# A two-layer hybrid transformer on one NeuronCore: experts interleaved on TensorE, attention and indexer heads in two row halves, a table scatter moved into a branch

## The chip, the core and the metric

One core of a Trainium2 chip. Everything is float32. The metric is the device time of one execution of the whole program in microseconds (us), smaller is better. TensorE (PE in the profile) multiplies, VectorE (DVE), ScalarE (ACT) and GpSimd (POOL) do the elementwise work, SyncE (SP) issues the large DMA loads, and POOL issues the indirect ones. SBUF is the on-chip memory, PSUM holds the results of TensorE in eight banks.

## The reference, cut to what matters

512 tokens of width 1024 pass two layers: a mixer, a layer norm, a mixture of experts, a layer norm and a gated injection. Layer 0 mixes by retention and pooling, which the change doesn't touch. Layer 1 mixes by sparse attention:

```python
sc = relu(einsum('bqhd,bsd->bqhs', q_idx, k_idx))     # indexer: 8 heads of 64
I = einsum('bqh,bqhs->bqs', w_idx, sc)                # causal; the top 128 keys are kept
logits = q . k * 64**-0.5 - slopes[h] * (t - idx)     # 16 heads of 64, kept keys alone
o = softmax(logits) @ v
```

Each layer's mixture has 32 experts of 1024 x 1024 (gate and up) and 512 x 1024 (down) weights; each token goes to two of them:

```python
h = xt[tok] @ w_gu[e];  a, b = split(h, 2)
y[row] += gate * ((silu(a) * b) @ w_down[e])
```

## The kernel before

The program is a list of blocks, each with one instruction stream for each engine and a barrier at its end: retention, output projection, routing (`route`), experts (`experts`), injection; then `latents` (indexer and latent projections of layer 1), `attention`, and again output projection, routing, experts, injection. Nothing is planned by a scheduler: the order on each engine is the order written, and semaphores join the engines.

**Experts.** Every expert gets 64 slots. SP streams the weights of an expert into one of two areas q = 0, 1 (experts 2i+q): three loads of 2 MB, the two halves of the gate and up weights (gu) and the down weights (dn). The loads of the next expert of an area are written in the order gu half 0, gu half 1, dn of q = 0, then the same of q = 1, and each waits for the matmuls that free its place (`s_gu_half`, `s_gu`, `s_dn`). Experts 0, 1 and the gate and up weights of expert 31 (in w3, w4) are in place before the block; the down weights of expert 31 come by `load_last_dn` into XT, once the second gather has landed. The last four places of the sequence run experts 31, 28, 29, 30. `one(q, i)` is written alike for TensorE, ScalarE and VectorE, and takes one expert from start to end on each before the next:

- TensorE transposes the gathered rows (L875), multiplies gate and up in two halves (L890), transposes the gated product (L897), multiplies down (L904). A token row is split in two column halves, which run in the two halves of TensorE's columns.
- ScalarE copies the transposed rows (L909), does silu (L913) and scales the result (L1195). VectorE multiplies (L916) and copies the transposed product (L919).
- GpSimd gathers a row list by indirect DMA (L863) and scatters the result (L869).

Before its second round of gathers GpSimd also writes `table` (L1120): eight indirect scatters of 128 entries of 16 bytes, which only the branch for overfull experts (`Further`, more than 64 tokens) reads. The branch isn't entered with this input: the trace holds 64 results of experts (L1195), 32 for each layer.

**Latents.** TensorE multiplies four chunks of indexer queries (L1468), and after them the scores of two heads for three row tiles (L1478). Key and query tiles hold two heads in 128 partitions; KI is kept twice, each with the other head's half zeroed, so that a score product contracts 128 rows. Two PSUM banks take the scores in turn. ScalarE rectifies (L1552), VectorE accumulates (L1616), then picks the top 128 (L1631, L1635) while TensorE goes on with the latents (L1508) and the projections (L1537).

**Attention.** 64 units (t, h): row tile t with (t + 1) * 128 keys, head h. A unit is a score product on TensorE (L1707, again 128 rows with zeroed halves of QH, two banks), slope and mask on VectorE (L1752), the row maximum (L1755), exp on ScalarE (L1775), the reciprocal on VectorE (L1739), the division on GpSimd for even units (L1795) and on VectorE for odd ones (L1745), transposes on TensorE (L1716), a copy on ScalarE (L1783) and, for two heads together, the product with the values (L1728). Transposes run 4 units and value products 6 units behind the scores.

## Time and profile before

| | us |
|---|---|
| median of three runs | 1728.17 (1726.48 to 1731.79) |
| the profiled execution | 1732.38 |
| its span, first to last instruction | 1730.5 |
| PE busy in it | 1455.4 |
| experts of layer 0, first to last product | 255.4 to 742.6 |
| experts of layer 1 | 1149.6 to 1635.9 |
| latents and attention | 838 to 1057 |

The profiled execution has 1.9 us around its span and is 4.2 us above the median, so that differences are taken from it and set against the median. DMA rates count all 16 engines of the core. A timeline row gives the start, the duration, the engine, the line and operation, the operands and the count of merged instructions; in brackets stands the idle time before it and what ended that. A float32 product of up to 512 columns shows as two MATMUL records.

### The profile page before, as it was taken

Reading aid. Unit: us, or ns where it says so; the run is one execution under the profiler, and the core shown is the slowest. Engines: PE = TensorE matmul, PEld = TensorE weight load, DVE = VectorE, ACT = ScalarE, POOL = GpSimd, SP = SyncE. Lnnn points to the kernel's source line nnn. Section 1 sums busy time; section 2 is a strip of 40 time slices with the busy share of each in tenths; the row PEclk is TensorE's granted clock in tenths of the full one; section 3 lists DMA queues with packets and bytes.
Section 4 is the critical chain, followed back from the end, with each engine's and each line's share of the span. In section 5 each row is a group of like instructions: output and inputs, shape, how many; then the busy total and the mean of one; then the engine's idle time right before and its main releaser. Section 6 shows DMA issues by size and latency. Waiting matters only on the chain. (4 is left out here: it accounts for less than half of the span.)

```text
span 1730.5 us, 16759 instructions
## 1 busy us (share of the span) xinstructions
PE 1455.4 (84%) x5992; PEld 662.9 (38%) x5992; DVE 407.3 (24%) x972; ACT 317.1 (18%) x656; POOL 219.7 (13%) x319
## 2 busy tenths in 40 slices
PE   7998968877877878869999999968878778788698
PEld 5885542222222223234444565532222222222243
DVE  3425340000000000044167584330000000000062
ACT  3211011101011010122234673011010100101121
POOL 0000012111111111100001241031111111111000
PEclk9999969999999999989999999969999999999989
DMA  7108159999999999854200004389999999999450
GB/s 271 49 25 333 67 195 294 428 429 430 427 429 430 429 428 429 327 222 179 103 0 1 1 1 189 122 243 384 429 429 428 430 429 429 429 429 410 200 207 37
DMA packets 78808, 482.44 MB, mean 279 GB/s; under 512 B 18912, under 2 KB 20964, under 8 KB 45992
## 3 DMA queue, kind: packets, MB, share of 16 engines
q1 hardware_dynamic: 65800, 463.76, 66.0%
q0 software_dynamic: 10752, 16.85, 2.7%
q10 hardware_dynamic: 2208, 1.20, 0.2%
q8 instruction: 28, 0.46, 0.1%
q14 instruction: 20, 0.16, 0.0%
HBM read 474.91 MB, written 23.63 MB: 288 GB/s over the span
## 5 line engine op out<-in xcount | busy, mean ns | idle before, releaser
L890 PE MATMUL PS<-wide,w 128*64 128x512 f32 x1984 | 454.9, 604 | 83.7 <-ACT w L909 44.5
L890 PEld LDWEIGHTS PS<-wide,w 128*64 128x64 f32 x1984 | 134.5, 138 | 361.7 <-issue 225.0
L904 PE MATMUL PS<-slim,w 128*64 128x512 f32 x992 | 238.4, 624 | 38.8 <-DVE w L919 38.8
L916 DVE TENSOR_TENSOR w<-w,PS 128x256 f32<-128x256 f32 x64 | 27.0, 421 | 872.5 <-ACT w L913 872.5
L904 PEld LDWEIGHTS PS<-slim,w 128*64 128x64 f32 x992 | 75.5, 142 | 158.8 <-issue 109.1
L913 ACT ACTIVATE w<-PS 128x256 f32<-128x256 f32 x64 | 24.6, 384 | 511.3 <-PE PS L890 511.3
L1305 PE MATMUL PS<-wide,XT 128*128 128x512 f32 x256 | 111.5, 592 | 0.0
L1195 ACT ACTIVATE w<-PS,w 128x512 f32<-128x512 f32 x64 | 44.0, 687 | 360.8 <-PE PS L904 360.8
L1112 POOL COPY w<-w 128x1 uint32 (+1 forms) x64 | 11.7, 183 | 702.0 <-ACT w L1195 702.0
L897 PE MATMUL PS<-ident,w 128*128 128x128 f32 x128 | 32.3, 334 | 60.2 <-DVE w L916 54.5
L863 POOL DMA_INDIRECT w<-x_rows,w x64 | 67.6, 1056 | 56.9 <-POOL w L1105 55.6
L869 POOL DMA_INDIRECT y_rows<-w x64 | 65.2, 1019 | 55.1 <-POOL w L1112 55.1
L1305 PEld LDWEIGHTS PS<-wide,XT 128*128 128x128 f32 x256 | 48.0, 190 | 57.4 <-issue 57.4
L897 PEld LDWEIGHTS PS<-ident,w 128*128 128x128 f32 x128 | 20.1, 206 | 116.5 <-DVE w L916 116.5
L637 PE MATMUL PS<-wide,slim 128*128 128x512 f32 x128 | 56.0, 594 | 1.1 <-PEq L1698 1.1
L875 PEld LDWEIGHTS PS<-ident,w 128*128 128x128 f32 x256 | 36.0, 209 | 54.3 <-issue 49.6
L875 PE MATMUL PS<-ident,w 128*128 128x128 f32 x256 | 48.6, 313 | 3.5 <-DMA w<-x_rows,w 3.5
L1707 PE MATMUL PS<-w,wide 128*128 128x128 f32 (+3 forms) x128 | 48.1, 460 | 1.5 <-PEq L1458 0.9
L169 ACT ACTIVATE XT<-PS 128x512 f32<-128x512 f32 x40 | 21.7, 594 | 139.5 <-PE PS L162 139.5
L1795 POOL TENSOR_SCALAR w<-w 128x128 f32<-128x128 f32 (+3 forms) x32 | 35.5, 1110 | 91.6 <-DVE w L1739 91.6
L405 PE MATMUL PS<-x_high,w_high 128*128 128x512 f32 x96 | 38.2, 398 | 7.9 <-DVE w_low L343 7.9
L909 ACT ACTIVATE w<-PS 128x512 f32<-128x512 f32 x64 | 37.8, 591 | 31.9 <-PE PS L875 31.8
(221 smaller groups left out, 1545.8 us busy)
## 6 DMA issues: line engine op xcount, KB each, us to landing
wide<-in_moe_w_gu SPq DMA_DIRECT2D x124, 2048.0 KB, 26.5
slim<-in_moe_w_down SPq DMA_DIRECT2D x62, 2048.0 KB, 26.6
w<-in_moe_w_gu SPq DMA_DIRECT2D x4, 2048.0 KB, 19.4
w<-y_rows SPq DMA_DIRECT2D x16, 512.0 KB, 9.1
wide<-in_ple_w_gate SPq DMA_DIRECT2D x4, 2048.0 KB, 13.6
w<-in_ab_w_in SPq DMA_DIRECT2D x2, 2048.0 KB, 13.9
w_in<-in_ab_w_in SPq DMA_DIRECT2D x2, 2048.0 KB, 7.7
x_rows<-X SPq DMA_DIRECT2D x8, 512.0 KB, 3.0
```

Of the source, the lines that this page charges most:

```text
L405: m = pe.matmul(PS[:, j % 8, :], lhsT, rhs, start=(k == 0 and r == 0), stop=(k == KD - 1 and r == 2))
L637: m = pe.matmul(PS[:, 2 * t + c, :], mixed[:, k, t * P:(t + 1) * P], w_halves[c][:, k, :], start=(k == 0), stop=(k == KD - 1))
L863: pool.indirect_dma_start(out=xg[q], out_offset=None, in_=x_half, in_offset=bass.IndirectOffsetOnAxis(ap=index, axis=0), bounds_check=2 * ...
L869: pool.indirect_dma_start(out=y_rows, out_offset=bass.IndirectOffsetOnAxis(ap=index, axis=0), in_=ys[q], in_offset=None, bounds_check=4 * ...
L875: m = pe.transpose(PS[:, q, c * P:(c + 1) * P], xg[q].rearrange("p (f c) -> p c f", c=4)[:, c, :], ident[:, :])
L890: m = pe.matmul(PS[u * SLOTS:(u + 1) * SLOTS, 2 + q, :], xeT[q][:, k, :], gu[k].rearrange("p (a u c) -> p a u c", a=2, u=2)[:, :, u, :], s ...
L897: m = pe.transpose(PS[:, 4 + q, c * P:(c + 1) * P], ga.rearrange("p (f c) -> p c f", c=2)[:, c, :], ident[:, :])
L904: m = pe.matmul(PS[u * SLOTS:(u + 1) * SLOTS, 6 + q, :], gT[:, k, :], dn[k][:, u * NB:(u + 1) * NB], start=(k == 0), stop=(k == FF // P - 1))
L909: return act.activation(xeT[q].rearrange("p (u c) s -> p c u s", u=2), PS[:, q, :].rearrange("p (c u s) -> p c u s", c=4, u=2), ACT.Copy)
L1195: act.activation(ys[q], PS[:, 6 + q, :], ACT.Copy, scale=R["gate_of"][:, bass.ds(expert(q, i), 1)]).then_inc(s_y[q], 1)
L1305: m = pe.matmul(PS[:, 2 + u % 6, :], XT[:, k, t * P:(t + 1) * P], wg[:, k, c * NB:(c + 1) * NB], start=(k == 0), stop=(k == KD - 1))
L1707: pe.matmul(PS[:, j % 2, 0:width[t]], QH[:, h % 2, h // 2, t * P:(t + 1) * P], KH[:, h // 2, 0:width[t]], start=True, stop=True).then_inc( ...
```

## The change

- `experts`: TensorE and ScalarE take two experts interleaved. Where TensorE had `one(0, i)`, `one(1, i)`, it now runs `up(0,i)`, `out(1,i-1)`, `back(0,i)`, `turn(1,i)`, `up(1,i)`, `out(0,i)`, `back(1,i)`, `turn(0,i+1)`. The streams of VectorE, of SP's expert loads and of GpSimd's gathers and scatters keep their order.
- The eight table scatters move into the branch for overfull experts. `load_last_dn` moves into the routing block, without its wait.
- `latents`: KI is kept once; the two heads of a chunk are multiplied in rows 0 to 63 and 64 to 127; the scores take four banks, and the two heads of a tile follow one another. Four zeroings on GpSimd go.
- `attention`: QH too is kept once and score products contract 64 rows; four score banks; slope, mask and maximum in one VectorE instruction (`tensor_tensor_reduce`), with the sign and slope folded into QH's scale; transposes 6 and value products 8 units behind; GpSimd divides three units of four, VectorE copies one transposed unit of four.

```diff
 # route
+                @block.sync
+                def _(sp):
+                    load_last_dn(sp, l)
 # experts, SP
-                    sp.wait_ge(s_gath[1], 16)
-                    load_last_dn(sp, l)
 # experts, GpSimd: moved into further.pool(pool, more, fill_table)
-                    pool.wait_ge(s_place, 1)
-                    for c in range(2 * T):
-                        pool.indirect_dma_start(
-                            out=table, ...).then_inc(s_tab, 16)
 # experts, TensorE (ScalarE: gate(0,i), scale(1,i-1), take(1,i), gate(1,i), scale(0,i), take(0,i+1))
-                        one(0, i)
-                        one(1, i)
+                    def pair_of(i, first=False):
+                        up(0, i)
+                        if not first:
+                            out(1, i - 1, first=isinstance(i, int) and i == 1)
+                        back(0, i)
+                        turn(1, i)
+                        up(1, i)
+                        out(0, i, first)
+                        back(1, i)
 # latents
-            units = [(t, h) for h in range(IH) for t in SEL]
+            units = [(t, 2 * c + u) for c in range(IH // 2) for t in SEL for u in range(2)]
-                            if i >= 2:
-                                pe.wait_ge(s_relu, i - 1)
-                            pe.matmul(PS[:, 6 + i % 2, 0:width[t]], QI[:, h // 2, t * P:(t + 1) * P],
-                                      KI[:, h % 2, 0:width[t]], start=True, stop=True).then_inc(s_is, 1)
+                            if i >= 4:
+                                pe.wait_ge(s_relu, i - 3)
+                            hd = slice((h % 2) * HD, (h % 2 + 1) * HD)
+                            pe.matmul(PS[:, 4 + i % 4, 0:width[t]], QI[hd, h // 2, t * P:(t + 1) * P],
+                                      KI[hd, 0:width[t]], start=True, stop=True).then_inc(s_is, 1)
 # attention
-            LAG_R, LAG_T, LAG_V = 1, 4, 6
+            LAG_R, LAG_D, LAG_T, LAG_V = 2, 3, 6, 8
+            divider = [1 if j % 4 == 3 else 0 for j in range(N)]
+            copier = [1 if j % 4 == 1 else 0 for j in range(N)]
+                                pe.matmul(PS[:, j % 4, 0:width[t]], QH[hd, h // 2, t * P:(t + 1) * P],
+                                          KH[hd, h // 2, 0:width[t]], start=True, stop=True).then_inc(s_s, 1)
-                        dve.scalar_tensor_tensor(g, DMASK[t], -slope[h], PS[:, i % 2, 0:width[t]],
-                                                 ALU.mult, ALU.add).then_inc(s_l, 1)
-                        dve.tensor_reduce(nmax[:, i:i + 1], g, AX.X, ALU.max, negate=True).then_inc(s_max, 1)
+                            dve.tensor_tensor_reduce(LG[i % LGS][:, 0:width[t]], PS[:, i % 4, 0:width[t]], DMASK[t],
+                                                     SLOPE[h], -LOWEST, ALU.add, ALU.min,
+                                                     nmax[:, i:i + 1]).then_inc(s_l, 1)
```

## Rows read from the trace of the kernel before

**Rows 1.** Page, span in 40 equal slices of 43 us: DMA busy in tenths, rate.

```profile
DMA  7108159999999999854200004389999999999450
GB/s 271 49 25 333 67 195 294 428 429 430 427 429 430 429 428 429 327 222 179 103 0 1 1 1 189 122 243 384 429 429 428 430 429 429 429 429 410 200 207 37
```

**Rows 2.** Busy time by windows: an expert stretch, and attention's last tile.

```profile
core 0: us, PE busy (x) PEld busy (x) DVE busy (x) ACT busy (x) POOL busy (x), PEclk, DMA share, GB/s
300.00:400.00 100.00, 80.05 (x360) 27.17 (x358) 5.07 (x12) 10.46 (x20) 17.16 (x28) 1.00 1.01 428
...
1020.00:1048.00 28.00, 28.00 (x199) 17.40 (x200) 24.53 (x55) 20.08 (x49) 12.39 (x8) 1.00 0.01 1
```

**Rows 3.** Timeline, layer 0: second gate-and-up halves of experts 3 and 27.

```profile
305.19 3.65 PE L890 MATMUL PS<-wide,w 128*64 128x512 f32 x16 [0.38 <-DMA wide<-in_moe_w_gu]
...
675.02 3.65 PE L890 MATMUL PS<-wide,w 128*64 128x512 f32 x16 [0.88 <-DMA wide<-in_moe_w_gu]
```

**Rows 4.** Timeline, end of layer 0's experts: expert 28, and the last down product.

```profile
701.73 7.09 PE L890 MATMUL PS<-wide,w 128*64 128x512 f32 x32 [0.69 <-ACT w L909]
...
709.75 0.50 PE L897 MATMUL PS<-ident,w 128*128 128x128 f32 x2 [0.94 <-DVE w L916]
...
710.77 3.65 PE L904 MATMUL PS<-slim,w 128*64 128x512 f32 x16 [0.52 <-DVE w L919]
...
738.91 3.65 PE L904 MATMUL PS<-slim,w 128*64 128x512 f32 x16 [0.52 <-DVE w L919]
```

**Rows 5.** Timeline, start of layer 0's experts: first and last table scatter, loads.

```profile
253.99 1.02 POOL L1120 DMA_INDIRECT table<-w  x1 [0.30 <-issue]
...
255.40 9.95 PE L890 MATMUL PS<-wide,w 128*64 128x512 f32 x32 [0.69 <-ACT w L909]
255.46 0.38 SPq L442 DMA_DIRECT2D XT<-in_moe_w_down  x1
...
262.17 3.77 SPq L429 DMA_DIRECT2D wide<-in_moe_w_gu  x2
...
262.98 0.96 POOL L1120 DMA_INDIRECT table<-w  x1 [0.31 <-issue]
...
271.20 0.39 SPq L433 DMA_DIRECT2D slim<-in_moe_w_down  x1
```

**Rows 6.** DMA view of 244 to 284 us, 40 slices of 1 us; median landing.

```profile
DMA  9999300040409175999999866998999716999559
GB/s 426 410 442 385 147 0 8 0 135 4 127 2 115 16 115 205 451 419 405 247 223 107 66 66 66 148 115 99 99 82 98 82 33 296 353 201 111 107 213 426
...
table<-w POOLq DMA_INDIRECT x8, 11.8
```

**Rows 7.** Table scatters of layer 0 (240 to 330 us), issue to landing.

```profile
DMA to landing us min/median/max: 4.4/11.8/18.7
```

**Rows 8.** Timeline, latents: score stretches, and the next long stretch.

```profile
858.03 2.68 PE L1478 MATMUL PS<-w 128*128 128x256 f32 x8
...
862.58 7.03 PE L1468 MATMUL PS<-XT,wide 128*128 128x512 f32 x16
...
880.86 2.68 PE L1478 MATMUL PS<-w 128*128 128x256 f32 x8
...
890.32 27.63 PE L1508 MATMUL PS<-wide,XT 128*128 128x512 f32 x64
```

**Rows 9.** Timeline, attention: first scores of t = 1, 2, 3, value products, last pair.

```profile
979.60 0.70 PE L1707 MATMUL PS<-w,wide 128*128 128x256 f32 x2
...
997.49 0.91 PE L1707 MATMUL PS<-w,wide 128*128 128x384 f32 x2
...
1020.71 1.12 PE L1707 MATMUL PS<-w,wide 128*128 128x512 f32 x2
...
1033.85 1.09 PE L1728 MATMUL PS<-w,XT 128*64 128x128 f32 x16
...
1046.32 1.13 PE L1707 MATMUL PS<-w,wide 128*128 128x512 f32 x2
```

**Rows 10.** Groups by line and form: the row maximum at 512 keys.

```profile
L1755 DVE TENSOR_REDUCE w<-w 128x1 f32<-128x512 f32 x16 | 11.0, 686 | 0.5
```

More of the change, by code:

```diff
@@ L998, in dve, with pool @@
                 self.run(dve, count, body, s["dve"], before)
-            def pool(self, pool, count):
+            def pool(self, pool, count, before):
                 s = self.s
@@ L1006, in body @@
                     scatter(pool, 1, put1[1], s["scat"])
-                self.run(pool, count, body, s["pool_end"])
+                self.run(pool, count, body, s["pool_end"], before)
             def pe(self, pe, count):
@@ L1132, in _, with fill_table, turn, up @@
                             put_rows(q, i)
-                    pool.wait_ge(s_tab, 16 * 2 * T)
                     for q in range(2):
                         pool.wait_ge(s_scat[q], 16 * PAIRS)
-                    further.pool(pool, more)
+                    def fill_table():
+                        pool.wait_ge(s_place, 1)
+                        for c in range(2 * T):
+                            pool.indirect_dma_start(
+                                out=table, out_offset=bass.IndirectOffsetOnAxis(ap=R["place"][:, c:c + 1], axis=0),
+                                in_=R["entry"][:, c, :], in_offset=None).then_inc(s_tab, 16)
+                        pool.wait_ge(s_tab, 16 * 2 * T)
+                    further.pool(pool, more, fill_table)
                 @block.tensor
                 def _(pe):
-                    def one(q, i, first=False):
-                        a, loads = area(q, i)
+                    def turn(q, i):
                         pe.wait_ge(s_gath[q], 16 * i + 16)
                         turn_gathered(pe, q).then_inc(s_turn[q], 1)
+                    def up(q, i):
+                        a, loads = area(q, i)
                         pe.wait_ge(s_xe[q], i + 1)
@@ L1150, in one, with back, out @@
                             gate_up(pe, q, last_gu if a is None else gu_of[a], half).then_inc(done[q], 1)
+                    def back(q, i):
                         pe.wait_ge(s_gated[q], i + 1)
                         turn_gated(pe, q).then_inc(s_gturn[q], 1)
+                    def out(q, i, first=False):
+                        a, loads = area(q, i)
                         pe.wait_ge(s_gt[q], i + 1)
@@ L1180, in _, with take, gate @@
                 def _(act):
-                    def one(q, i, first=False):
+                    def take(q, i):
                         act.wait_ge(s_turn[q], i + 1)
                         copy_gathered(act, q).then_inc(s_xe[q], 1)
+                    def gate(q, i, first=False):
                         act.wait_ge(s_gu[q], i + 1)
@@ L1189, in one, with scale @@
                         silu(act, q).then_inc(s_silu[q], 1)
+                    def scale(q, i, first=False):
                         act.wait_ge(s_dn[q], i + 1)
@@ L1196, in one, with pair_of @@
                                        scale=R["gate_of"][:, bass.ds(expert(q, i), 1)]).then_inc(s_y[q], 1)
-                    one(0, 0, first=True)
-                    one(1, 0, first=True)
+                    def pair_of(i, first=False):
+                        gate(0, i, first)
+                        if not first:
+                            scale(1, i - 1, first=isinstance(i, int) and i == 1)
+                        take(1, i)
+                        gate(1, i, first)
+                        scale(0, i, first)
+                    take(0, 0)
+                    pair_of(0, first=True)
+                    take(0, 1)
+                    pair_of(1)
                     more = further.count(act)
-                    with act.Fori(1, END) as i:
-                        one(0, i)
-                        one(1, i)
+                    with act.Fori(2, END) as i:
+                        take(0, i)
+                        pair_of(i)
                     for i in (END, END + 1):
-                        one(0, i)
-                        one(1, i)
+                        take(0, i)
+                        pair_of(i)
+                    scale(1, END + 1)
                     further.act(act, more)
@@ L1421, in build @@
         m8 = {1: w2[:, 3376:3384], 2: w2[:, 3384:3392], 3: w2[:, 3392:3400]}
+        SLOPE = [2.0 ** (-8.0 * (h + 1) / AH) for h in range(AH)]
         SEL = list(range(1, T))
```

170 lines of the change are left out of this document (82 added, 88 removed).

## The prediction

> **What bounds the kernel now.** I read the page's slices first: in two long stretches the DMA engines are busy throughout at 429 GB/s, and between them lies a stretch with hardly any transfer [rows 1]. The windows say who works there. In the experts TensorE is busy 80 of 100 us while the DMA share is 1.01: the weight stream is the bound. In the last tile of attention TensorE is busy 28.0 of 28 us, VectorE 24.5, ScalarE 20.1, GpSimd 12.4: TensorE is the bound, VectorE close behind [rows 2].
>
> The timeline gives the two rates that matter in the experts. From the second gate-and-up half of expert 3 to that of expert 27, both released by a landing weight load, are 369.8 us for 24 experts: 15.4 us each, or 5.14 us for each 2 MB load with the gathers and scatters beside it [rows 3]. Where no load is waited for, at the end, two experts lie between the down products at 710.77 and 738.91: 14.07 us each [rows 4]. So TensorE's own rate is only 1.3 us better than the stream's, and a TensorE order that is faster still gains nothing in the middle. It can gain at the two ends alone: when the stream starts, and after it stops.
>
> **Experts, middle.** In the interleaved order the idle 0.93 us before L897 (the wait for silu and product) and 0.52 us before L904 [rows 4] lie behind another expert's product. The wait for the copied rows (0.69 us) stays, since turn still stands directly before up. TensorE's own rate becomes 14.07 - 0.93 - 0.52 = 12.6 us an expert, under 15.4: worth 0 here. The cover for that is the DMA stream; without it the edit would give 1.45 us an expert.
>
> But the order of releases changes, and SP's order doesn't. A dn place used to be free about 6 us after its expert's second half; now out(q) runs after the other expert's up. With the second half of expert (0,i) landing at 0: half 3.65, out(1,i-1) to 7.3, back and turn and copy, first half of the next at 10.3 (its load landed), second half at 15.4 (load) to 19.1, out(0,i) to 22.7. Only then may SP issue dn(0), and the two gu halves behind it in SP's queue, whose places have been free for some us, go with it. The stream works until 30.8 on what was issued before (expert (0,i+1)'s halves end there), so the three loads arrive some 8 us before the queue is dry. The same margin holds for the other area. I take 0, and keep the dry queue as a rival.
>
> **Experts, start.** Here is the largest single thing in the trace. From 263 to 282 us the DMA engines are busy and move only about 140 GB/s, 20 slices that sum to 2812 GB/s of a possible 8600 [rows 6]; 13.5 us of stream are lost. The table scatters are issued from 254.0 to 263.0 [rows 5] and take up to 18.7 us to land, hence until about 281.7 [rows 7]: the slow stretch ends as they do. The gathers and scatters of every expert run in the middle too, at 428 GB/s [rows 2], so they aren't the cause. With the table out, the stream runs at 5.14 us a load, and the releases decide. The first up starts at 255.4, its first half frees its place at 262.2, its end is at 265.35 [rows 5]. Then wait and back to 266.8, turn and copy 1.4 to 268.2, up(1,0) 7.1 to 275.3, out(0,0) to 279.0, against a dn load issued at 271.2 before. The two gu halves of expert 2 land by about 274, the queue is dry until 279.0, and three loads from about 280.5 end at 296 to 296.5: the second half of expert 3 is there, which before started at 305.19 [rows 3, 5]. Gain 8.7 us, I take 8.5 for each layer (layer 1 has the same eight scatters), 17 in all. Bounds: 0 if the slow stretch stays; 15.8 if the queue never went dry (262.2 + 1.5 + 5 x 5.14 = 289.4).
>
> `load_last_dn` in routing adds 5 us of stream there. The engines are idle from 249 [rows 6], so it moves into empty time, until about 253. The first gathers now share the engines with it and TensorE waits for the first of them (L875): I put 1 us on it for each layer, bounds 0 and 2, loss 2 in all. GpSimd loses eight scatters, which frees its gather of the third expert, not waited for.
>
> **Experts, end.** After up of expert 27, before: 0.93 + 0.5 + 0.52 + 3.65, then four experts of 14.07: 61.9 us to the end of the last down. After: out of 26 and back 4.15, four of 12.7, then 0.5 and the last out 3.65: 59.1 [rows 4]. The last dn load is released after out(1,14) and still lands 7 us before its use. Gain 2.8 a layer, 5.6 in all. Bounds: 0 (a late last load) and 4.3.
>
> **Latents.** A single full-row product costs 27.63/64 = 0.43 us for each record, 0.86 at 512 columns [rows 8]. The four chunks of scores cost TensorE 4.55, 4.55 and 9.46 us (862.58 - 858.03; 890.32 - 880.86). Two heads in two row halves should run at once, as the two column halves of the value products do: 16 records of 128 columns in 1.09 us, where one after the other at 0.107 they would take 1.7 [rows 9]. A chunk is 2304 columns; at half, 1.9 us and some 0.2. But ScalarE and VectorE have to follow, with two relu tiles: I put chunks 0 and 1 at 3.0 each, and 2 and 3 together at 6.5: 3.1 + 3.0 = 6.1 less. VectorE's selection starts that much earlier, nearly, so the third wait in the latents moves along; I take 5.5, bounds 2 and 7. The zeroings were on GpSimd beside longer TensorE work: 0.
>
> **Attention.** A pair of units takes (997.49 - 979.60)/8 = 2.24 us at t = 1, 2.90 at t = 2, and (1046.32 - 1020.71)/7 = 3.66 at t = 3 [rows 9]. Two heads at once save half of four records, less 0.06 for one more switch of the tile shape: at t = 3 0.80, t = 2 0.58, t = 1 0.37; at t = 0, where the engines wait for one another, I take 0.2 to 0.3. Eight pairs of each: 6.4 + 4.6 + 3.0 + 2.0 = 16. The others must keep up with the 2.86 us a pair at t = 3, which is 22 us for what the window of 28 us holds. VectorE drops a reduction of 0.69 us for each of its 15 units [rows 10], 24.5 - 10.3, plus a few copies: 15. GpSimd's half becomes three quarters: 12.4 x 1.5 = 18.6. ScalarE gives copies away: under 20.1. All fit, GpSimd and ScalarE narrowly. The deeper lags add one round of transposes and value products at the end, 1 us. Gain 15. What the fused instruction costs, no row shows: between one pass (0.69) and two (1.37) [rows 10]. At two, VectorE would need 25 us of the window and bind: 5 us of the 15 gone. I take one pass, as it reads each operand once. Bounds of the whole term: 0 (row halves don't overlap) and 20 (the four banks also remove the waits at t = 0 and 1).
>
> What a change of tile shape costs is seen at the value products, which have one at either end: 1.09 us for 16 records, of which 8 slots of 0.107 are 0.86, so at most 0.23 for switches and the pipeline's tail together [rows 9]. The Trainium skill speaks against this part: its page TensorEngine Tiling (Array Packing), section Key Properties, says that changing the tiling mode, unlike changing the tile, drains TensorE. By the row the term stays at 15; by the rule, with a drain of 0.23 at each end of every pair of scores, 36 pairs would lose up to 16 and nothing would be left, which is the second rival's end.
>
> **Sum.** 17 - 2 + 5.6 + 5.5 + 15 = 41 us off the profiled 1732.4 (span 1730.5 and 1.9 around it), hence 1691 for such an execution; the median of before is 4.2 lower, so 1728.2 - 41 = 1687.
>
> **Rivals.**
> - The slow stretch stays, since something else in it is slow (the load into XT, the first results): nothing is gained at the starts, 1728.2 - 24 = 1704. For it: the last load was in flight there too. Against: it ends as the last table scatter lands. The Trainium skill, page DMA: Bandwidth & Descriptors, section Specifications, has transfers under 512 B done by read-modify-write, and the scatter's entries have 16 B; the trace agrees with the forecast's side, by the 140 GB/s. 0.10.
> - The row halves don't overlap, or the switch or the fused instruction eats it: latents and attention give 2 to 5 instead of 20, 1710. For it: no row shows row halves. Against: the column halves. 0.13.
> - The engines keep step better than I count (four banks, longer lags), 50 to 60 less: 1673. 0.10.
> - Slower: the queue of loads runs dry in the middle, as dn and the next two halves now go out together. Of 58 streamed experts each has to lose 0.71 us to cancel the 41; at 1.0 us the time is 1728 - 41 + 58 = 1745. Against: 8 us of margin. 0.06.
> - The forecast: 0.61.
>
> **How the numbers follow.** The forecast's own range is 1675 to 1700, from the bounds of its terms. To hold 8 of 10 the range takes in the first two rivals nearly, and a part of the third: 1668 to 1708. A difference under 0.3% (5 us) is about what a measurement of this kernel can't tell from none. Faster by more than that: the first, second, third and last case, less their tails, 0.90. Slower by more: 0.05, the dry queue. Within: 0.05.
>
> **What would show it.** In the DMA slices no stretch of busy engines at 100 to 200 GB/s after the first expert; the second half of expert 3 some 41 us after the first up started, instead of 50; in the middle 15.4 us an expert, DMA share 1.0; down products at the end some 12.7 us apart; pairs in attention of 2.9 us at t = 3; L1508 about 6 us earlier after the first L1468. The prediction is wrong if a slow stretch remains, if the middle takes more than 15.6 us an expert, or if score pairs last as long as before.

## The result and the profile after

The changed kernel takes 1711.24 us against 1729.98 us for the kernel before on the same chip (medians of 4 each), a ratio of 0.989 with a 95% interval of 0.986 to 0.992. It is faster, by 19 us where 41 were forecast (1687, range 1668 to 1708), so the time lies above the range. One execution of the four took 2482 us at a granted clock of 0.55 and is left out of the ratio; the median of the other three is 1709.62.

The profiled execution took 1709.62 us (span 1707.7). Its page, the slices that answer to [rows 1] and the clock above them:

```profile
PEclk8999969999999999989999699969999999999989
DMA  7107267999999999883200004378999999999650
GB/s 275 50 26 306 100 240 290 429 430 428 427 425 428 427 428 423 328 312 129 104 1 1 1 2 178 124 304 360 430 429 428 427 424 426 426 413 421 255 209 37
```

The two streams are as fast as before, and the clock line of the changed kernel has a 6 at slice 22 (from 939 to 982 us), counted from 0. The other two 6s are in the page of before too, where slice 22 has a 9.

**Start of the experts.** The DMA view of 244 to 284 us, 40 slices of 1 us, as [rows 6]:

```profile
DMA  9999999984000030009399999999910000098999
GB/s 442 426 410 442 426 426 418 434 357 164 0 0 0 0 90 0 0 0 229 98 393 442 410 459 426 426 459 393 393 66 16 0 0 0 0 147 336 401 410 459
```

The stretch at 140 GB/s is gone. The last down load fills the time to 253. Between 274 and 279 the queue is dry. The timeline of TensorE, then of SyncE's queue, as [rows 5]:

```profile
254.27 1.13 PE L879 MATMUL PS<-ident,w 128*128 128x128 f32 x4 [4.12 <-DMA w<-x_rows,w]
256.09 8.61 PE L894 MATMUL PS<-wide,w 128*64 128x512 f32 x32 [0.69 <-ACT w L913]
...
274.24 3.60 PE L908 MATMUL PS<-slim,w 128*64 128x512 f32 x16
...
292.77 8.78 PE L894 MATMUL PS<-wide,w 128*64 128x512 f32 x32 [0.69 <-ACT w L913]
```

```profile
278.08 0.39 SPq L433 DMA_DIRECT2D slim<-in_moe_w_down  x1
278.77 1.35 SPq L429 DMA_DIRECT2D wide<-in_moe_w_gu  x2
```

The first row shows a wait of 4.12 us for the first gather. The same row of the kernel before:

```profile
253.58 1.13 PE L875 MATMUL PS<-ident,w 128*128 128x128 f32 x4 [1.87 <-DMA w<-x_rows,w]
```

In layer 1 the wait is 3.39 us, and was 1.12. The moved load is in flight as the gather is issued; v_lastdn below tests that it is the cause. Expert 3's up ends at 301.55, so its second half began about 3.65 earlier, at 297.9, 41.8 us after the first up (49.8 before).

**Middle and end of the experts.** Timeline of TensorE, as [rows 3, 4]:

```profile
399.34 8.75 PE L894 MATMUL PS<-wide,w 128*64 128x512 f32 x32 [2.17 <-DMA wide<-in_moe_w_gu]
407.92 3.60 PE L908 MATMUL PS<-slim,w 128*64 128x512 f32 x16
411.46 0.51 PE L901 MATMUL PS<-ident,w 128*128 128x128 f32 x2
...
712.85 7.09 PE L894 MATMUL PS<-wide,w 128*64 128x512 f32 x32 [0.69 <-ACT w L913]
719.77 3.60 PE L908 MATMUL PS<-slim,w 128*64 128x512 f32 x16
723.30 0.50 PE L901 MATMUL PS<-ident,w 128*128 128x128 f32 x2
724.32 3.65 PE L908 MATMUL PS<-slim,w 128*64 128x512 f32 x16 [0.52 <-DVE w L923]
```

Transposes and down products have lost their waits, save the last; the saved time is now the wait for the load, and a part of it goes into a lower clock (0.94 from 300 to 400 us, 1.00 before), which the stream covers. The last down product ends 14.6 us earlier than before (727.97 against 742.56). Of that 1.7 us is no effect of the change: in the profiled execution of before one down product of this stretch took 5.35 us instead of 3.65, at a granted clock of 0.83 from 680 to 690 us:

```profile
680.93 5.35 PE L904 MATMUL PS<-slim,w 128*64 128x512 f32 x16 [0.82 <-DVE w L919]
```

**Latents**, as [rows 8]: the score chunks (the first and the last two together are shown) take 2.5, 2.5 and 6.79 us between long products, where they took 4.55, 4.55 and 9.46.

```profile
845.71 2.57 PE L1520 MATMUL PS<-w 64*128 64x256 f32 x12
848.21 7.13 PE L1509 MATMUL PS<-XT,wide 128*128 128x512 f32 x16
...
864.83 6.86 PE L1520 MATMUL PS<-w 64*128 64x256 f32 x24
871.62 3.70 PE L1550 MATMUL PS<-wide,XT 128*128 128x512 f32 x8
```

**Attention.** Windows (columns as in [rows 2], the granted clock is the figure before the DMA share) of its first part, and of its last tile:

```profile
940.00:960.00 20.00, 17.39 (x69) 8.68 (x67) 5.32 (x44) 11.16 (x40) 3.35 (x9) 0.89 0.00 0
960.00:980.00 20.00, 18.67 (x81) 9.33 (x80) 8.05 (x48) 9.55 (x38) 4.29 (x10) 0.50 0.00 1
...
1020.00:1048.00 28.00, 24.88 (x226) 16.67 (x225) 12.56 (x42) 15.91 (x35) 6.70 (x9) 1.00 0.06 7
```

From 960 to 980 us TensorE ran at its lower level, 1.2 GHz; before, the clock was 1.00 throughout. The timeline at t = 3, as [rows 9]:

```profile
1025.52 1.13 PE L1749 MATMUL PS<-w,wide 64*128 64x512 f32 x4
1026.58 1.09 PE L1758 MATMUL PS<-ident,w 128*128 128x128 f32 x8
1027.60 1.09 PE L1770 MATMUL PS<-w,XT 128*64 128x128 f32 x16
1028.62 1.13 PE L1749 MATMUL PS<-w,wide 64*128 64x512 f32 x4
1029.68 0.66 PE L1758 MATMUL PS<-ident,w 128*128 128x128 f32 x4
1031.29 0.63 PE L1758 MATMUL PS<-ident,w 128*128 128x128 f32 x4 [0.95 <-DVE w L1782]
1031.85 1.09 PE L1770 MATMUL PS<-w,XT 128*64 128x128 f32 x16
1032.87 1.13 PE L1749 MATMUL PS<-w,wide 64*128 64x512 f32 x4
```

Four score records now take what two took. One pair goes through in 3.10 us, the next in 4.25, with a wait for a PSUM copy of VectorE in it (L1782). Such waits sum to 9.0 us in attention.

The spans of the two profiled executions differ by 22.8 us; that is 4 more than the medians, since the one of before is above its median and the one of the changed kernel below. The table splits them at the starts of six TensorE records in the two timelines (first up of layer 0; its last down; first and last score of attention; first up of layer 1; its last down; and the end of the span):

| stretch | before | after | difference | forecast |
|---|---|---|---|---|
| up to the first up | 255.4 | 256.1 | +0.7 | +1 |
| experts, layer 0 | 486.6 | 471.3 | -15.3 | -11.3 |
| injection, latents | 225.4 | 223.3 | -2.1 | -5.5 |
| attention's scores | 80.7 | 82.7 | +2.0 | -15 |
| last values, layer 1's start | 101.4 | 105.3 | +3.9 | +1 |
| experts, layer 1 | 485.8 | 474.8 | -11.0 | -11.3 |
| rest | 95.2 | 94.2 | -1.0 | 0 |

The terms for the experts were met or passed, the one for attention missed by 17 and the one for the latents by 3.4. The first experiments ask where each lies.

### The profile page after: what moved, and what is told of

Read it like the earlier page. It is cut to its first block and busy times, and to the rows that moved or that the text cites. A ratio compares the mean times of both kernels' runs of the same rounds, so it can differ in the third digit from the quotient of the medians.

```text
span 1707.7 us, 16740 instructions
## 1 busy us (share of the span) xinstructions
PE 1453.6 (85%) x5992; PEld 670.6 (39%) x5992; DVE 379.9 (22%) x972; ACT 315.9 (18%) x640; POOL 188.0 (11%) x315
## 5 line engine op out<-in xcount | busy, mean ns | idle before, releaser
L894 PE MATMUL PS<-wide,w 128*64 128x512 f32 x1984 | 499.4, 655 | 148.6 <-DMA wide<-in_moe_w_gu 138.8
L894 PEld LDWEIGHTS PS<-wide,w 128*64 128x64 f32 x1984 | 157.2, 149 | 448.4 <-issue 364.1
L908 PE MATMUL PS<-slim,w 128*64 128x512 f32 x992 | 223.6, 592 | 1.0 <-DVE w L923 1.0
L923 DVE COPY w<-PS 128x256 f32<-128x256 f32 x64 | 27.2, 425 | 188.6 <-PE PS L901 188.6
L879 PE MATMUL PS<-ident,w 128*128 128x128 f32 x256 | 42.8, 291 | 10.5 <-DMA w<-x_rows,w 10.5
L1834 POOL TENSOR_SCALAR w<-w 128x128 f32<-128x128 f32 (+3 forms) x48 | 26.5, 554 | 136.3 <-DVE w L1798 135.9
L1818 ACT ACTIVATE w<-w 128x128 f32<-128x128 f32 (+3 forms) x64 | 35.6, 556 | 31.9 <-DVE w L1792 31.9
L879 PEld LDWEIGHTS PS<-ident,w 128*128 128x128 f32 x256 | 36.8, 210 | 11.5 <-DMA w<-x_rows,w 11.5
## 6 DMA issues: line engine op xcount, KB each, us to landing
wide<-in_moe_w_gu SPq DMA_DIRECT2D x124, 2048.0 KB, 17.9
slim<-in_moe_w_down SPq DMA_DIRECT2D x62, 2048.0 KB, 13.4
```

Of the source, the lines that this page charges most:

```text
L879: m = pe.transpose(PS[:, q, c * P:(c + 1) * P], xg[q].rearrange("p (f c) -> p c f", c=4)[:, c, :], ident[:, :])
L894: m = pe.matmul(PS[u * SLOTS:(u + 1) * SLOTS, 2 + q, :], xeT[q][:, k, :], gu[k].rearrange("p (a u c) -> p a u c", a=2, u=2)[:, :, u, :], s ...
L908: m = pe.matmul(PS[u * SLOTS:(u + 1) * SLOTS, 6 + q, :], gT[:, k, :], dn[k][:, u * NB:(u + 1) * NB], start=(k == 0), stop=(k == FF // P - 1))
L923: return dve.tensor_copy(gT.rearrange("p (u c) s -> p c u s", u=2), PS[:, 4 + q, 0:2 * P].rearrange("p (c u s) -> p c u s", c=2, u=2))
L1818: act.activation(g, g, ACT.Exp, bias=nmax[:, i:i + 1], scale=-1.0, accum_out=rsum[:, i:i + 1]).then_inc(s_p, 1)
```

## The experiments

Each time below is the median of its executions, with the ratio to the kernel before on the same chip. That kernel's median there was 1732.4 for the four runs whose names begin with e, 1731.7 for v_serial, v_sporder, v_lastdn and v_copyfirst, 1730.9 for v_repeat, v_pool_one, b_two and b_all, and 1731.1 for the last three. Durations of stretches are read as in the table, from one profiled execution each. How far they can be trusted is seen at b_all and b_all_repeat below: the experts' code is the same, and their experts differ by 3 us a layer.

### One part of the change at a time

e_experts is the changed kernel with the latents and attention of before, e_attention the kernel before with the changed latents and attention. e_table is the kernel before with one edit:

```
# e_table, GpSimd, before.py + this only
-  pool.wait_ge(s_place, 1)
-  for c in range(2 * T): pool.indirect_dma_start(out=table, ...)
...
-  pool.wait_ge(s_tab, 16 * 2 * T)
+  def fill_table(): ...      # called in the branch for overfull experts
-  further.pool(pool, more)
+  further.pool(pool, more, fill_table)
```

> The part of the changed kernel up to the injection (start, experts, routing with the table in its branch) with the latents and attention of the kernel before. Theory (the experts' part works nearly as forecast, attention gives its share back): 15.3 + 10.9 = 26 us of the two layers' experts less 3 us of a shorter lead at the injection, so 23 us below before, 1705 us (1702 to 1710). Rival (the experts gain less and attention does pay something): 12 us below, 1716 us.

> The experts and routing of the kernel before with the latents and attention of the changed one. Theory: the latents' chunks give 6 us, attention itself takes 4 us more, so 2 us below before, 1726 us (1722 to 1731), with TensorE at half clock in the first 20 to 25 us of attention and every second pair waiting about 0.9 us for VectorE's copy. Rival (attention was slow only because of what ran ahead of it, the half clock came from the shorter experts): attention 9 us shorter than in the changed kernel and the whole 1716 us.

> The kernel before with one edit: the scatters of the table are in the branch for overfull experts. Theory (the slow stretch of the DMA queues at the start of each layer's experts was the cost, and the order of the experts on TensorE is worth little in itself): 13 to 20 us a layer less, 1688 to 1702 us, and no stretch at 140 GB/s. Rival as I had it in the prediction (table 17 us in two layers, interleaved order another 6): 1711 us.

| | median | ratio (95%) | experts | scores of attention |
|---|---|---|---|---|
| e_experts | 1712.92 | 0.990 (0.988 to 0.992) | 472.1, 475.3 | 81.5 |
| e_attention | 1727.09 | 0.997 (0.996 to 0.998) | 486.2, 485.3 | 80.1 |
| e_table | 1702.91 | 0.984 (0.982 to 0.985) | 471.4, 473.2 | 81.6 |

One edit alone beats the whole change by some 8 us. Its DMA view of 244 to 284 us:

```profile
DMA  9996104030759999695999999998999999999999
GB/s 451 426 426 254 74 0 127 12 121 6 115 147 393 426 434 418 254 279 229 459 393 426 426 410 475 393 410 377 385 385 377 397 426 496 389 422 492 385 426 459
```

There is no slow stretch and no dry one, and the experts take 471.4 and 473.2 us. The second half of expert 27 starts 406.2 us after the first up in layer 0 (419.6 before) and 408.2 in layer 1 (420.7 before), 13.4 and 12.5 us earlier, so nearly all of the 13.5 us of stream that the prediction found lost in [rows 6] comes back in each layer. (The whole stretches are 15.2 and 12.6 shorter, the first with the 1.7 us of the slow down product of before.) The interleaved order with the moved load adds nothing to that: e_experts's experts are no shorter. What the interleave gives after expert 27 (a tail of 57.5 us in the changed kernel, 62.2 in e_table) it has lost by then (expert 27's second half starts at 410.7 against 406.2).

The time of e_experts, 1713 us, lies between its theory and its rival. What it loses against e_table, 8.1 us of span, is the later first up of layer 0 (3.1 us), that of layer 1 (2.2) and 0.7 and 2.1 us in the experts.

e_attention has the time of its theory, 5 us better, but not its parts: the latents give 4.3 us and not 6, and attention's scores take no 4 us more but 0.6 less. The granted clock in the first 20 us of scores was as low as the changed kernel's (0.62 from 961 to 981 us, 0.61 from 951 to 971 there), with the old experts ahead of it. With the old attention it was 0.91 in e_experts and e_table. So the half clock belongs to the changed attention and not to what runs before it. VectorE's copies are waited for as in the changed kernel, 9.2 us in all.

### The order of the experts, the loads, the last down weights

v_serial is the changed kernel with TensorE's and ScalarE's serial order of before. v_sporder keeps the interleaved order and gives SyncE an order to match (the loads of the last four experts, left out here, follow the same pattern):

```
-  with sp.Fori(1, END) as i:
-      for q in range(2): half 0 of (q,i); half 1 of (q,i); down of (q,i)
+  both_halves(0, 1); both_halves(1, 1); down_of(0, 1)
+  with sp.Fori(2, END) as i:
+      both_halves(0, i); down_of(1, i - 1); both_halves(1, i); down_of(0, i)
```

v_lastdn puts `load_last_dn(sp, l)` back behind `sp.wait_ge(s_gath[1], 16)`.

> The changed kernel with TensorE's and ScalarE's orders of the experts as they were before (turn, up, transpose and down of one expert behind one another). Theory (what the experts gained comes from the table alone, and the interleave costs: the kernel before with only the table out ended 9 to 10 us earlier than the one with the whole experts' part changed): 9 us below the changed kernel, 1702 us. Rival (the loss of those 10 us sits in the early load of the last down weights, which delays the gathers, and the orders are equal): 1711 us, as the changed kernel.

> The changed kernel with SyncE's loads in the order in which the interleaved TensorE frees the buffers (halves of gate and up of one expert, then the down weights of the one before it). Theory (the interleave loses because SyncE waits in the old order, at the start of a layer for about 5 us with empty queues and in each pair of experts little): the dry gap around 30 us after the first product goes, 4 to 5 us a layer, 1702 us. Rival (the gap is taken back in the middle, where the DMA bound sets the pace and clock dips are hidden): 1708 to 1711 us.

> The changed kernel with the last down weights loaded behind the gathers, where they were. Theory (the load holds the first gather up by 2.2 us in each layer, and the loads behind it are not needed earlier): 0 to 4 us below the changed kernel, 1709 us. Rival (the load was off the path and now stands in the stream of the first loads: 5 us later for each of the loads behind it, 5 us a layer more): 1720 us.

| | median | ratio (95%) | experts | first up of layer 0 |
|---|---|---|---|---|
| v_serial | 1702.75 | 0.983 (0.982 to 0.984) | 473.3, 472.8 | 256.6 |
| v_sporder | 1696.89 | 0.979 (0.976 to 0.981) | 468.1, 468.7 | 256.0 |
| v_lastdn | 1702.95 | 0.983 (0.981 to 0.984) | 474.7, 475.5 | 254.0 |

v_serial had the time of its theory, but not for its reason: its experts took as long as the interleaved ones, and the profiled execution was 4.8 us shorter in attention's scores, whose code is the same (the granted clock after the first 20 us was 1.00 there, from 971 to 1029 us, and 0.91 in the changed kernel, from 971 to 1034), and 2.6 us shorter between the experts and attention. So in the experts the interleaved order, as it stands, is worth nothing and costs nothing. Whether it costs clock in what follows is open: with this attention code the two kernels with serial experts took 77.9 and 80.1 us (v_serial, e_attention), and the three with interleaved ones 82.5 to 82.7 (the changed kernel, v_sporder, v_lastdn).

v_sporder gains 3.2 and 6.1 us in the experts, more than its theory's 4 to 5 a layer in one of them, and the dry slices from 274 to 279 are gone (98 to 459 GB/s there). A gain of 3 us in one execution is at the limit of what can be read, but b_two and b_all below have it in both layers (b_all_repeat in one alone). The spans differ by 11.5 us; of the rest 3.0 lie between the last down product and attention, where v_serial, with the same code, is 2.6 us shorter as well, so they aren't put down to this edit.

In v_lastdn the first gather's wait is back at 1.77 us (1.14 in layer 1), so the moved load was its cause, and the first up is 2.1 us earlier:

```profile
252.19 1.13 PE L875 MATMUL PS<-ident,w 128*128 128x128 f32 x4 [1.77 <-DMA w<-x_rows,w]
254.00 4.53 PE L890 MATMUL PS<-wide,w 128*64 128x512 f32 x10 [0.69 <-ACT w L909]
```

The experts of layer 0 take 3.4 us longer (0.7 in layer 1), so with the dry queue still there the move is nearly neutral in the trace (span 1704.8 against 1707.7), while its median is 8 us lower; that larger difference is across two measurements and I don't rest on it.

### Attention: the copies

e_copies_act and v_copyfirst change who makes the PSUM copies, and when:

```
# e_copies_act
-  copier = [1 if j % 4 == 1 else 0 for j in range(N)]
+  copier = [0 for j in range(N)]
# v_copyfirst, VectorE
   for i in range(N + LAG_T + 2):
+      j = i - LAG_T - 1
+      if 0 <= j < N and copier[j] == 1: copy_turned(dve, dve.tensor_copy, j)
       if i < N: ... tensor_tensor_reduce ...
       ...
-      (the same two lines here)
```

> The changed kernel with all PSUM copies of attention on ScalarE. Theory (the 0.93 us waits of every second pair are for VectorE's copy, which stands behind its fused product): those waits go, attention 9 us shorter, 1702 us. Rival (ScalarE, with exponentials of about 0.7 us a unit, becomes what the pairs wait for): waits of the same size behind ScalarE, 1708 to 1716 us.

> The changed kernel with VectorE's PSUM copy issued ahead of its fused product and row sum in each iteration of attention, instead of behind it. Theory (the wait of 0.93 us of every second pair is that fused product, 0.69 us, with its read of the sum): the waits shrink to below 0.3 us and attention is 6 to 9 us shorter, 1703 us. Rival (the copy waits for the transposes anyway and then holds up the fused product, which the normalisation needs): as the changed kernel or 3 us more, 1711 to 1714 us.

e_copies_act: 1697.34 us, 0.981 (0.979 to 0.982), scores 71.2 us. v_copyfirst: 1699.77 us, 0.981 (0.980 to 0.983), scores 71.7 us. Both take 11 us out of attention, 2 more than their theories had, and both theories stand. Not all of the 11 us is the wait, though: the granted clock after the first 20 us was also higher (0.98 and 0.96, against 0.91). e_attention has the same attention code as the changed kernel, and its clocks (0.62, then 0.96) are those of v_copyfirst (0.60, then 0.96): against its 80.1 us the copies' part is 8.4 to 8.9 us, about the 9.0 us of waits. What TensorE's transposes waited for in v_copyfirst, with idle us and times:

```profile
  issue: 12.4, 25
  POOL w L1834: 7.2, 11
  ACT w L1737: 2.2, 4
```

VectorE is no longer in the list. In the changed kernel it held up the whole ring, the tiles and banks that the engines hand from one to the next: the copy of unit j stands behind the fused product of unit j+7, whose scores TensorE issues directly ahead of the transposes that need the copy's bank. TensorE then waits for a product and a copy of VectorE in a row.

### Attention: the clock

v_repeat is v_copyfirst with the scores of t = 0 issued three times into the same bank:

```
+  for _ in range(3 if t in (0,) else 1):
       m = pe.matmul(PS[:, j % 4, 0:width[t]], ...)
+  m.then_inc(s_s, 1)
```

> The version with VectorE's copy first, with the score products of the first row block of every head issued three times (the same result written again), so that TensorE has more to do in the first 25 us of attention. Theory (the half clock there follows the idle time of TensorE as attention starts, so work in the gaps keeps the full clock): the granted clock in the first 20 us of attention rises from 0.73 to over 0.9 and attention becomes 3 to 5 us shorter, 1696 us. Rival (the clock falls for another reason, the form or the amount of the small products among them): clock 0.7 to 0.8 as before and 1 to 2 us more for the added products, 1701 us.

1694.82 us, 0.981 (0.979 to 0.982); scores 67.9 us. Windows of the first 20 us of attention and the rest, v_copyfirst and then v_repeat:

```profile
952.00:972.00 20.00, 18.66 (x93) 9.98 (x90) 9.92 (x76) 13.11 (x59) 5.89 (x15) 0.60 0.01 1
972.00:1023.00 51.00, 49.48 (x401) 29.46 (x401) 32.98 (x141) 37.17 (x110) 18.29 (x30) 0.96 0.01 2
```

```profile
949.00:969.00 20.00, 18.64 (x172) 12.96 (x172) 11.80 (x84) 14.89 (x64) 6.86 (x17) 1.00 0.01 1
969.00:1017.00 48.00, 46.15 (x387) 27.57 (x388) 31.54 (x133) 35.95 (x105) 17.32 (x28) 1.00 0.01 2
```

More work for TensorE made attention shorter: the clock went from 0.60 to 1.00 and the scores' stretch from 71.7 to 67.9 us, added products included. The half clock thus depends on how much TensorE is given as the changed attention starts; their form alone isn't the cause, since more products of the same form brought the clock back. In the whole time the gain can't be told from none: the two ratios' intervals overlap.

By row tile, in us from the first score of a tile to that of the next (of t = 3 to the last score). The forecast is the time before less the prediction's gain for the tile:

| | before | changed | v_serial | v_copyfirst | v_repeat | forecast |
|---|---|---|---|---|---|---|
| t = 0 | 12.2 | 11.9 | 11.9 | 11.5 | 11.3 | 10.2 |
| t = 1 | 17.9 | 23.5 | 18.7 | 19.0 | 15.4 | 14.9 |
| clock at t = 1 | 1.00 | 0.57 | 0.82 | 0.65 | 1.00 | |
| t = 2 | 23.2 | 22.0 | 22.0 | 19.7 | 19.7 | 18.6 |
| t = 3 | 27.4 | 25.3 | 25.3 | 21.6 | 21.6 | 21.0 |

At t = 2 and 3 the clock is 1.00 in all five, and the copies' order alone costs 2.3 and 3.7 us. At t = 1 it and the clock cost 8.1 us together (23.5 against 15.4), of which the clock at least 4.8, since v_serial has the same attention code.

### Attention: GpSimd's division

The changed kernel also gives GpSimd's division a second operand, a factor of 1.0. The list of the change doesn't name this, and the prediction didn't count it. v_pool_one takes it out:

```
-  pool.tensor_scalar(g, g, rden[:, i:i + 1], 1.0, ALU.mult, ALU.mult)
+  pool.tensor_scalar(g, g, rden[:, i:i + 1], None, ALU.mult)
```

> The changed kernel with GpSimd's division in its one-operand form again (times the reciprocal, no second factor of 1). Theory (the second operand is what more than halves its time, 1656 to 741 ns at 512 columns, and the unit is otherwise the same): GpSimd's instruction takes 1.66 us again at 512 columns, and with three quarters of the divisions on GpSimd it becomes the bound of attention, 2.2 us a pair at most, 5 to 10 us more, 1717 us. Rival (the instruction got fast because VectorE uses its port less in the changed kernel): 0.74 us as in the changed kernel and 1711 us.

1706.70 us, 0.986 (0.985 to 0.988); scores 83.1 us. GpSimd by form, of the changed kernel and of v_pool_one:

```profile
L1834 POOL TENSOR_SCALAR w<-w 128x512 f32<-128x512 f32 x12 | 8.9, 741 | 17.7 <-DVE w L1798 17.7
```

```profile
L1834 POOL TENSOR_SCALAR w<-w 128x512 f32<-128x512 f32 x12 | 19.1, 1609 | 9.2 <-DVE w L1798 9.2
```

The first half of the theory held: the form alone more than doubles GpSimd's time. The second did not. The kernel got no slower. GpSimd still waits 9.2 us for reciprocals at t = 3, and VectorE's copies remained what TensorE waited for (9.2 us). The edit of that line bought nothing in this kernel. Whether it does once the copies are out of the way, where GpSimd is what the transposes wait for (7.2 us in v_copyfirst), no run shows.

### Together, and what the row halves are worth

b_two has SyncE's matched order and all copies on ScalarE; b_all the last down load behind the gathers as well; b_all_repeat also the scores of t = 0 three times. c_serial is b_all_repeat with the serial order on TensorE, ScalarE and SyncE. c_one_half is b_all_repeat without the odd heads' own scores: both heads of a pair are computed from rows 0 to 63, so that its output isn't the layer's:

```
-  hd = slice((h % 2) * HD, (h % 2 + 1) * HD)
+  hd = slice(0, HD)
```

> The changed kernel with two edits: SyncE's loads in the order of the releases, and all PSUM copies on ScalarE. Theory (both gains are measured alone, 6 to 10 us in the experts' loads and 11 us in attention, and lie one behind the other): 1684 us (1680 to 1690). Rival (the earlier end of one stage is given back by a lower clock in the next): 1692 us.

> The version before this one in the list with the last down weights loaded behind the gathers as well. Theory (the load in front of the gathers costs 2.4 us a layer, and the freed loads behind do not need it early): 5 us less than the version with the two edits, 1680 us. Rival (with SyncE in the right order the early load fills the queues while nothing else can be loaded, and moving it back costs 2 to 3 us a layer, as the experts' 3.2 us more in layer 0 with that edit alone): 1686 to 1689 us.

> The version with the three edits (loads in the order of the releases, all PSUM copies on ScalarE, last down weights behind the gathers), and the score products of the first row block issued three times, which kept TensorE's clock at 1.00 in attention. Theory (the half clock at the start of attention costs 4 us net): 1680 us, attention 67 us. Rival (ScalarE, with all copies, is what the first blocks wait for at full clock): attention 71 us as without, 1684 us.

> As the version with the four edits, but with the experts in the serial order of before on TensorE, ScalarE and SyncE (turn, up, transpose and down of one expert behind one another; SyncE's loads in the order that goes with it). Theory (the interleaved order gains only the 3 to 5 us a layer by which its experts with matched loads, 467 us, beat the serial ones, 472 us): 9 us slower than that version, 1689 us. Rival (the orders are equal once the last down weights are behind the gathers, since the DMA engines set the pace in both): within 3 us of it.

> As the version with the four edits, but the scores of the odd heads are computed from the rows of the even heads (0 to 63 for both), so that both products of a pair lie in one row half; the odd heads' own scores are left out. Theory (two heads in different row halves overlap, 4 records in 1.13 us, and in one half they do not): 2.2 us for a pair of 512 columns, 0.8 to 1.07 us a pair more at t=3, less at narrower blocks (some 0.25, 0.5, 0.8 at 128, 256, 384), so 8 pairs by 2.6 and the twice added products of t=0: attention 18 to 22 us longer. Rival (the time of four records is the same in one half, the saving being the 64 instead of 128 rows): attention within 2 us.

| | median | ratio (95%) | experts | scores |
|---|---|---|---|---|
| b_two | 1686.74 | 0.975 (0.974 to 0.976) | 466.8, 469.9 | 71.0 |
| b_all | 1683.63 | 0.973 (0.972 to 0.974) | 467.8, 468.1 | 70.9 |
| b_all_repeat | 1683.62 | 0.971 (0.970 to 0.973) | 471.1, 470.9 | 68.0 |
| c_serial | 1685.95 | 0.974 (0.973 to 0.975) | 471.2, 472.9 | 67.9 |
| c_one_half | 1697.00 | 0.980 (0.979 to 0.982) | 467.6, 471.4 | 82.4 |

The gains add up to the time that the prediction gave the change: b_all and b_all_repeat, at 1684, beat both kernels. b_two is within its theory's range. b_all is 3 us below b_two: less than the 5 of its theory, and not above b_two as its rival had it. b_all_repeat has the shorter attention of its theory (68.0 us) and the time of its rival. Its profiled execution, the slowest of its five, has longer experts; by the medians, on two chips, the repeated products are worth nothing that can be seen. c_serial is 2 us slower than b_all_repeat by the medians and 5 by the ratios, whose intervals touch at 0.973, and its experts are no longer than those (471.2 and 472.9 against 471.1 and 470.9): a gain of the interleaved order in the whole kernel isn't shown, even with matched loads. The rival of c_serial stands. One score stretch of a pair in one row half (c_one_half), and of the same pair in two (b_all_repeat):

```profile
1003.16 1.98 PE L1767 MATMUL PS<-w,wide 64*128 64x512 f32 x4
1005.07 0.88 PE L1777 MATMUL PS<-ident,w 128*128 128x128 f32 x6
```

```profile
1004.92 1.13 PE L1767 MATMUL PS<-w,wide 64*128 64x512 f32 x4
1005.99 0.33 PE L1777 MATMUL PS<-ident,w 128*128 128x128 f32 x1
```

Two row halves save 0.85 us of 1.98 for a pair at 512 keys, and 14.4 us in the scores' stretch. That is less than the 18 to 22 of its theory: by tile it is 3.7, 1.2, 3.5 and 6.0 us, where the theory had some 2, 4, 6.4 and 8.6. It is settled that halves overlap.

## Why the prediction was off

- **Start of the experts, 8.5 a layer: held in layer 0, too large in layer 1.** The slow stretch was the table's scatters. In layer 0 expert 3's second half began 41.8 us after the first up (forecast 41) and expert 27's came 8.9 us earlier after it than before; in layer 1 7.1 and 5.7 us earlier. The dry queue from 274 to 279 came where the prediction put it. What it didn't see is that this gap was a price of the order of loads: with the serial order nothing is dry, and nearly all of the 13.5 us come back. The prediction booked as a gain of the change what was left after the interleave had spent a third of it. Its sign, expert 3, doesn't measure the stream either: in e_table, where all of it comes back, expert 3's second half still begins 48.7 us after the first up (49.8 before), held by TensorE's own order, and the gain shows later.
- **Moved last down load, 1 a layer: too small.** The gathers wait 2.25 and 2.27 us longer; even the bound of 2 was passed. Putting it back costs the experts 3.4 and 0.7 us where the queue runs dry (v_lastdn), and 1.0 and -1.8 where it doesn't (b_all against b_two); there the kernel is better off with the load behind the gathers, by 3 us in all.
- **Middle, 0: held.** DMA share 1.01, 429 GB/s, pairs of experts 30.5 us apart (15.3 each). TensorE's shorter expert shows as a wait for loads.
- **End, 2.8 a layer: too small.** From the end of expert 27's up the tail took 57.5 us where 59.1 were forecast; before it had been 63.9, and not the 61.9 that I worked out, by the down product of 5.35 us. In layer 1, without such a product, it was 61.9 before and 56.8 after, 5.1 less. So the interleave gave more at the end than was forecast, and this covers what the starts lacked.
- **Latents, 5.5: the chunks gave more, the stretch less.** The chunks take 11.8 us where there were 18.6, 6.8 less. From the first indexer product to attention's first score 4.3 us of it are left, also in e_attention; where the rest went I haven't traced; the granted clock behind the chunks was 0.86 from 900 to 925 us, and 0.93 before in the same place (918 to 943). Another 2.2 us are lost ahead of them, from the last down product to the first indexer product (103.4 us against 101.2), at a mean clock of 0.90 instead of 0.93. So 2.1 show.
- **Attention, 15: the step that failed.** Its terms for TensorE came near. Pairs at t = 3 without a wait take 3.10 us (2.86 forecast, 3.66 before), and the fused instruction is one pass of 0.69 us. Without the copy wait and with the clock at 1.00 the scores take 67.9 us against 80.7 before, 12.8 less. What failed is the sentence that the others must "keep up" and "All fit": I compared busy times of a window and didn't lay out in what order VectorE meets its work. The busy times themselves were below the forecast (in the 25.3 us of t = 3 VectorE 14.0 for 15, and GpSimd 7.4 for 18.6, by the second operand that I hadn't counted), and still VectorE held the others up. Its copy stands behind a fused product that needs scores issued just ahead of the transposes that need that copy's bank. That ring costs 0.95 us in every second pair, 9.0 us of waits, and 8.4 to 8.9 us by the runs at like clocks. The second loss is the lower clock from about 955 to 980 us, at least 4.8 us at t = 1 by v_serial, and 3.8 us even with the copies in order, by v_repeat. With the repeated products added the clock was 1.00. The two losses together are the 14.8 us between 82.7 and 67.9. I had looked for a lower clock nowhere in attention.
- **The rivals.** The second one (row halves and latents give 2 to 5) gives 1710, near the measured time, but by luck. From its own terms, 17 - 2 + 5.6 and 2 to 5, follow 1703 to 1706 and not 1710, and its mechanism didn't happen: the halves do overlap, and c_one_half prices that. By the page TensorEngine Tiling (Array Packing) of the Trainium skill, section Key Properties, a change of the tiling mode drains TensorE. The trace neither shows nor excludes such a drain: a pair at t = 3 took 3.10 us and not 2.86, which leaves 0.24 us for it, where the price that the prediction put on the rule was 0.46 (over 36 pairs; attention has 32 pairs of scores). What the trace does show is that the overlap, 0.85 us a pair, is worth more.

## What to carry over

When engines hand tiles round in a ring, check the order of each engine's instructions against the issue order of the others, besides the busy times of a window: an engine that is half idle can still hold up a pair by one instruction that stands in the wrong place. An edit that changes the order in which buffers come free needs the order of the loads changed with it, and a load moved into idle time can delay a small transfer that the next step waits for, here the first gather by 2.25 us. Take a change apart before keeping it: here one of its parts alone was better than the whole. And where a stage misses its forecast, look at the granted clock before putting all of it down to a wait: here a part of the 11 us was clock.

## What the runs showed of the hardware

- Eight indirect scatters of 16-byte entries held the other queue's stream at 140 GB/s for 19 us. With them moved out, and nothing else changed, expert 27 came 13.4 and 12.5 us earlier after the first up.
- GpSimd's `tensor_scalar` with a second operand (times 1.0) took 741 ns at 128x512, and 1609 ns without one. The same holds at 128 columns (375 and 601).
- The fused add, scale and row minimum ran in one pass, 687 ns at 128x512, with a read of its result behind it:

```profile
L1792 DVE CUSTOM_DVE_ANT_0 w<-PS,w 128x512 f32<-128x512 f32 x16 | 11.0, 687 | 11.9 <-PE PS L1749 11.9
...
L1792 DVE DVE_READ_ACCUMULATOR2_ANT w<- 128x1 f32 x64 | 5.3, 83 | 0.0
```

- TensorE was granted 1.2 GHz (0.50) from 960 to 980 us in the changed kernel. With the copies in order the first 20 us of attention had 0.60, and with the first products issued three times besides 1.00, which is 2.4 GHz.
- Four 64-row score records of 512 columns took 1.13 us in two row halves and 1.98 us in one.
- A 2 MB load in flight lengthened the wait for the first small gather from 1.77 to 4.12 us.
